# The q, k, v projection joined to layer 0's block, with the attention's first loads beside the value products

## The reference, cut to what matters

```python
xs = layer_norm(ALPHA * xs + g2_s * fs, ln2_g[i], ln2_b[i])        # end of layer 0
hs = xs * (1.0 + sc1_s) + sh1_s                                     # modulation of layer 1
q, k, v = split_heads(h @ w_qkv)                                    # 1024 x 3072, 16 heads of 64
s_loc = einsum('bhrjqd,bhrjkd->bhrjqk', qb, kg) + bias              # window keys, relative position bias, mask
s_ctx = einsum('bhrjqd,bhkd->bhrjqk', qb, k_ctx)                    # 256 cached context keys
p = softmax(concatenate([s_loc, s_ctx]))
o = p[..., :nk] @ vg + p[..., nk:] @ v_ctx
```

## Time and profile before

| what | value |
|---|---|
| median of 3 runs | 3832.96 us (3830.51 to 3836.11) |
| the profiled execution, its own time | 3835.01 us |
| its span | 3833.2 us |
| TensorE matmuls busy | 3599.0 us, 94% of the span |
| mean granted clock of TensorE | 0.974 of full |
| last matmul of layer 0's feed-forward to the first projection matmul | 1943 to 1976.10 us |
| projection | 1976.10 to 2325.7 us |
| last value matmul to the first minimum of the attention | 2325.7 to 2355.61 us |

### The profile page before, as it was taken

The page is one execution under the profiler, slowest core; times in us unless marked ns, Lnnn a source line. Parts: engine busy times, 40 slices in busy tenths (PEclk is TensorE's granted clock), DMA queues, the critical chain, the costliest instruction groups (busy, mean ns, idle before and its releaser), DMA issues. The chain is left out here.

```text
span 3833.2 us, 47327 instructions
## 1 busy us (share of the span) xinstructions
PE 3599.0 (94%) x19244; PEld 3066.8 (80%) x19244; DVE 1515.4 (40%) x2472; ACT 1034.0 (27%) x1552; POOL 1229.6 (32%) x815
## 2 busy tenths in 40 slices
PE   8999998889999999999979996999899999999997
PEld 7788887667788888888858876888778888888886
DVE  2765553454434443344440013777331122211116
ACT  1441211132511111111242213777434111111113
POOL 1531113533522222222351212666253222222223
PEclk9999999899999999999989998999999999999998
DMA  3253324754122222222243436777211111111111
GB/s 117 94 171 111 106 88 159 241 170 149 45 66 67 81 68 72 66 66 66 72 146 134 150 124 177 172 180 178 88 34 33 39 39 39 39 34 39 39 39 61
DMA packets 178567, 369.58 MB, mean 96 GB/s; under 512 B 17048, under 2 KB 102552, under 8 KB 176697
## 3 DMA queue, kind: packets, MB, share of 16 engines
q1 hardware_dynamic: 172920, 356.21, 29.2%
q10 hardware_dynamic: 5440, 10.49, 0.9%
HBM read 286.93 MB, written 79.69 MB: 96 GB/s over the span
## 5 line engine op out<-in xcount | busy, mean ns | idle before, releaser
L147 POOL TENSOR_TENSOR w_lo<-w_raw,w_hi 128x1024 fp32r<-128x1024 f32 x210 | 505.6, 2408 | 1513.7 <-ACT w_hi L141 1513.7
L155 PE MATMUL ps_r<-a_hi,w_hi 128*128 128x512 f32 (+1 forms) x2112 | 539.3, 358 | 13.0 <-POOL a_lo L1440 10.6
L155 PE MATMUL ps_r<-a_hi,w_lo 128*128 128x512 f32 (+1 forms) x2112 | 535.8, 357 | 0.0
L155 PE MATMUL ps_r<-a_lo,w_hi 128*128 128x512 f32 (+1 forms) x2112 | 535.6, 357 | 0.0
L141 ACT ACTIVATE w_hi<-w_raw 128x1024 fp32r<-128x1024 f32 (+1 forms) x217 | 225.2, 1038 | 1024.9 <-PE ps_r L155 442.3
L155 PEld LDWEIGHTS ps_r<-a_hi,w_hi 128*128 128x128 f32 x2112 | 350.9, 188 | 84.0 <-POOL a_lo L1440 18.2
L155 PEld LDWEIGHTS ps_r<-a_hi,w_lo 128*128 128x128 f32 x2112 | 350.8, 188 | 62.5
L155 PEld LDWEIGHTS ps_r<-a_lo,w_hi 128*128 128x128 f32 x2112 | 350.9, 188 | 62.4 <-issue 1.0
L1632 DVE TENSOR_TENSOR hid_l<-hid_l,ps_r 128x1280 f32<-128x1280 f32 x44 | 65.5, 1488 | 843.0 <-PE ps_r L155 843.0
L1652 DVE SCALAR_TENSOR_TENSOR x_t_l<-ps_r,mod,x_t_l 128x1024 f32<-128x1024 f32 (+1 forms) x288 | 241.4, 880 | 266.0 <-PE ps_r L155 266.0
L1480 POOL TENSOR_TENSOR hid_lo_l<-hid_l,hid_hi_l 128x1280 fp32r<-128x1280 f32 x42 | 134.6, 3205 | 490.7 <-ACT hid_hi_l L1382 490.7
(11 more groups left out here) (232 smaller groups left out, 6517.7 us busy)
## 6 DMA issues: line engine op xcount, KB each, us to landing
w_raw<-in_w_all SPq DMA_DIRECT2D x213, 512.0 KB, 3.6
ada_w_l<-in_ada_t SPq DMA_DIRECT2D x59, 512.0 KB, 3.6
q_hl<-q_d SPq DMA_DIRECT2D x64, 320.0 KB, 5.9
v_hl<-v_d SPq DMA_DIRECT2D x128, 128.0 KB, 2.9
t_tail_f<-in_ada_t SPq DMA_DIRECT2D x24, 512.0 KB, 4.1
k_hl<-k_d SPq DMA_DIRECT2D x32, 384.0 KB, 8.8
spec<-gout_f SPq DMA_DIRECT2D x80, 128.0 KB, 2.1
g_spec_c<-spec ACTq DMA_DIRECT2D x20, 512.0 KB, 5.3
```

The source lines that it names most:

```text
L147: pool.tensor_tensor(wl[:, s, 0:width], raw[:, s, 0:width], wh[:, s, 0:width].bitcast(F32), ALU.subtract).then_inc(w_split, 1)
L155: last = pe.matmul(out[:, c0:c1], w[:, c % 2, blk * 128:blk * 128 + 128], x[:, c0:c1], start=start and b == 0 and term == 0, stop=stop and ...
```

## The change

The five engine parts of `stage_qkv` become functions (`qkv_parts`) that run at the end of `stage_rest(0)`'s own block, with tiles laid over those that the LayerNorm no longer needs. So no barrier stands between the two. The first two weights' products are made chunk by chunk: the first two chunks of both, then the third, which waits for `a_lo` k by k. ACT and POOL wait for the stores of x (`y_out`) before they write over `x_t`. The value blocks are taken in the order 8, 9, 0, ..., 7 (`VM`), so that the additional copies to `z_f` fall on the first four halves. After the third value block SP loads q, k and bias of the attention's first head, after the fourth, fifth and sixth a third of the mask each, which ACT converts. The last stores of v are no longer awaited at the end of the block, but by SP in the attention ahead of the loads of v. The attention's first head waits for no load, and its prologue on ACT runs one tiny exponential first. A few small tiles move into the arena, and the first head's q, k, mask and bias tiles are shared by the two stages. What is computed is the same.

```diff
+        def load_qk(sp, q, k, pair, hh, q_done, k_done):
...
+        def qkv_parts(st, e0, place, pg, px, n2, y_out):
+            vwh, vwl = [place(n, 32768 * b, [128, KT, D], F32R) for b, n in enumerate(("vw_hi", "vw_lo"))]
+            zf = place("z_f32", 65536, [128, 2, TOK])
+            zh, zl = [place(n, 75776 + 10240 * b, [128, 2, TOK], F32R) for b, n in enumerate(("z_hi", "z_lo"))]
+            zv = [place(f"z_v{n}", 76288 + 8192 * n, [128, 8, 2, 128], F32R) for n in range(2)]
+            pv = [px[:, 0:512], px[:, 512:1024]]
+            VM = (8, 9, 0, 1, 2, 3, 4, 5, 6, 7)
+            att = first_att(place)
...
+            def qkv_sp(sp):
+                sp.wait_ge(n2.acc, 24)
+                cache_in(0)
+                cache_in(1)
...
+                for n, m in enumerate(VM):
+                    sp.wait_ge(vl_ok, 2 * n + 2)
+                    sp.dma_start(v_d[128 * m:128 * m + 128, :, :, :], zv[n % 2].bitcast(F32)).then_inc(v_out[n % 2], 16)
+                    if n < 2:
+                        sp.wait_ge(vf_ok, 2 * n + 2)
+                        sp.dma_start(t["nv"][128 * m - LS:128 * m - LS + 128, :], zf[:, n, 0:1024]).then_inc(c_out, 16)
+                    if n == 2:
+                        for j in range(2):
+                            sp.wait_ge(z_out[j], 1 + 32 * 4 + 48 * 4)
+                        sp.wait_ge(c_out, 16 * 14)
+                        load_qk(sp, q0, k0, 0, 0, q_e, k_e)
+                        sp.wait_ge(w_split, EV + 10)
+                        load_bias(sp, bias, 0, 0, b_e)
+                    if 3 <= n < 6:
+                        if n > 3:
+                            sp.wait_ge(ms_ok, n - 3)
+                        sp.dma_start(m_raw[:, :], t["mask"].rearrange("p a b -> p (a b)")[:, 768 * (n - 3):768 * (n - 2)]
+                                     ).then_inc(ms_in, 16)
+                sp.wait_ge(q_e, 64)
+                sp.wait_ge(k_e, 32)
+                sp.wait_ge(b_e, 128)
...
+            def qkv_pool(pool):
+                pool.wait_ge(y_out, 16 * 24)
+                pool.wait_ge(n2.bc, 3)
...
+            def qkv_act(act):
+                act.wait_ge(y_out, 16 * 24)
...
+                for n in range(20):
+                    m, h = n // 2, n % 2
+                    if n in (12, 14, 16):
+                        c = n // 2 - 6
+                        act.wait_ge(ms_in, 16 * c + 16)
+                        act.activation(att[2].rearrange("p a b -> p (a b)")[:, 768 * c:768 * c + 768], m_raw[:, :],
+                                       ACT.Copy).then_inc(ms_ok, 1)
...
+                    if m < 2:
+                        act.activation(zf[:, m, 512 * h:512 * h + 512], pv[h][:, :], ACT.Copy).then_inc(vf_ok, 1)
...
+                    if m < 2:
+                        dve.wait_ge(vf_ok, n + 1)
...
+            def qkv_pe(pe):
+                pe.wait_ge(n2.acc, 24)
+                for j in range(2):
+                    pe.wait_ge(w_split, e0 + j + 1)
+                    if j:
+                        pe.wait_ge(n2.s2_ok, 21)
+                    for ci in range(2):
+                        pe.wait_ge(n2.lo, 8 * ci + 8)
+                        products(pe, e0 + j, [(k, a_h[:, k, :], a_l[:, k, :], pg[j]) for k in range(KT)],
+                                 (CHUNKS[ORDER[ci]],))
+                for j in range(2):
+                    for k in range(KT):
+                        pe.wait_ge(n2.lo, 16 + k + 1)
+                        last = products(pe, e0 + j, [(k, a_h[:, k, :], a_l[:, k, :], pg[j])], (CHUNKS[ORDER[2]],),
+                                        k == 0, k == KT - 1)
+                    last.then_inc(w_used, 1)
...
+                        c0 = 128 * VM[m]
+                        xh, xl = a_h[:, k, c0:c0 + 128], a_l[:, k, c0:c0 + 128]
...
@@ stage_rest, at the end of each engine's part
+                    if not last_layer:
+                        qkv_sp(sp)
...
-        def stage_qkv(e0):
...
-        stage_qkv(e0)
@@ the attention's stage
+            q0, k0, mask, bias = shared[0]
+            qq = [q0, place("q_hl1", 76288, [128, 2, TOK], F32R)]
+            kk = [k0, place("k_hl1", 86528, [128, 1536], F32R)]
...
-                load_qk(0, 0)
-                flat = t["mask"].rearrange("p a b -> p (a b)")
-                for n in range(2):
-                    if n:
-                        sp.wait_ge(mk_ok, 1)
-                    sp.dma_start(pb[:, :, :].rearrange("p a b -> p (a b)")[:, 0:1152],
-                                 flat[:, 1152 * n:1152 * n + 1152]).then_inc(m_in, 16)
-                    if n == 0:
-                        load_bias(0, 0)
+                for j in range(2):
+                    sp.wait_ge(v_out[j], 16 * 5)
                 for n in (0, 4, 1, 2, 3, 5):
                     load_v(0, n)
-                load_qk(0, 1)
-                load_bias(0, 1)
+                load_qk(sp, qq[1], kk[1], 0, 1, kq_in[1], kq_in[1])
+                load_bias(sp, bias, 0, 1, b_in[1])
...
+                    first = i * 96 + 96 * (u // U) + 96 * hh
+                    if u % 10 == 0 and first:
+                        pe.wait_ge(kq_in[hh], first)
...
                 def prologue():
-                    for n in range(2):
-                        act.wait_ge(m_in, 16 * n + 16)
-                        act.activation(mask[:, :, :].rearrange("p a b -> p (a b)")[:, 1152 * n:1152 * n + 1152],
-                                       pb[:, :, :].rearrange("p a b -> p (a b)")[:, 0:1152], ACT.Copy).then_inc(mk_ok, 1)
+                    act.activation(stat[:, 0, 3:4], eps[:, :], ACT.Exp)
...
-                    pool.wait_ge(mk_ok, 2)
```

More of the change, by code:

```diff
@@ L996, in hyena_natten_step, with first_att, names_of @@
         ORDER = (2, 0, 1)
+        shared = []
+        def first_att(place):
+            return (place("q_hl0", 92672, [128, 2, TOK], F32R), place("k_hl0", 70144, [128, 1536], F32R),
+                    place("mask", 65536, [128, 6, 384], BF16),
+                    nc.alloc_sbuf_tensor_at(names_of("rpb_t"), [128, 2, 16, RPB_W], F32, offset=base_w).ap())
+        def names_of(name):
+            names[0] += 1
+            return f"{name}_{names[0]}"
+        def load_qk(sp, q, k, pair, hh, q_done, k_done):
+            rows = slice(64 * hh, 64 * hh + 64)
+            for hl in range(2):
+                for half in range(2):
+                    sp.dma_start(q[64 * half:64 * half + 64, hl, :].bitcast(F32), q_d[hl, pair, rows, :]).then_inc(q_done, 16)
+            for hl in range(2):
+                sp.dma_start(k[64 * hl:64 * hl + 64, :].bitcast(F32), k_d[hl, pair, rows, :]).then_inc(k_done, 16)
@@ L1291, in _ @@
                     spread(n2, 2)
+                    if not last_layer:
+                        qkv_pe(pe)
                 @block.scalar
@@ L1895, in hyena_natten_step @@
+                    if not last_layer:
+                        qkv_dve(dve)
         stage_rest(0, e0)
         e0 += E_OUT + E_FFN
-        stage_qkv(e0)
         e0 += E_QKV
@@ L2057, in _ @@
                     load_v(i, 3)
-                    load_bias(i, 1)
+                    load_bias(sp, bias, i, 1, b_in[1])
             @block.tensor
@@ L2078, in scores @@
                         for hl in range(2):
-                            last = pe.matmul(dst, qq[:, hh, hl, c0:c0 + 128], keys, start=hl == 0, stop=hl == 1)
+                            last = pe.matmul(dst, qq[hh][:, hl, c0:c0 + 128], keys, start=hl == 0, stop=hl == 1)
                     last.then_inc(s_mm, 1)
@@ L2203, in bias_mask @@
                         pool.wait_ge(sm_ok, unit_at(i, u - 1))
-                    if u % 10 == 0:
-                        pool.wait_ge(b_in[hh], i * 128 + (128 * (u // U) + 128))
+                    first = i * 128 + 128 * (u // U) + 128 * hh
+                    if u % 10 == 0 and first:
+                        pool.wait_ge(b_in[hh], first)
                     x = BIAS_X[j]
```

431 lines of the change are left out of this document (192 added, 239 removed).

## The result

The changed kernel takes 3808.8 us as the median of five runs (3807.8 to 3812.5). The kernel before took 3836.1 beside it, the median of five (3830.5 to 3843.2). The ratio is 0.9931 [0.9918, 0.9944], so 27 us are gained where 34.45 were forecast, and the median lies 10 us above the forecast of 3798.6, at the very top of the range of 3791 to 3809. Repeated twice beside other kernels, the changed kernel had 3806.2 and 3810.2, the one before 3837.1 and 3837.0.

The account below looks back on a forecast made before the run. TensorE, busy 94% of the span, was taken as the bound, so only its idle time could be won. 12.2 - 0.55 + 25.6 - 2.8 = 34.45 us saved gave a median of 3798.6 us, range 3791 to 3809.

Parts of the forecast that it names:

- the low clock at the third tile: Projection's third tile, after PE's wait for its weight: a low-clock start was taken as 0, with 2.75 us as bound.
- the second head's late loads: Attention's change to the second head: v, q, k and bias queue behind the awaited store, 2.8 us lost, bounds 0 and 7.2.
- the third weight's low part will end at 1994.65: First border: cache chain and third weight's load shift earlier together; third tile starts at 1994.65 instead of 2006.85, 12.2 us saved.
- the wait of 2.55 us: Projection: PE, done with two tiles at 1992.1, waits 2.55 us for the third weight until 1994.65.
- The value products: Value products: an extra copy lengthens the wait ahead of the third half, 0.55 us lost; new loads hide at no cost.
- The second border: Value products to attention: first minimum at about 2330.0 instead of 2355.61, 25.6 us saved, last-copy part included.
- at 231 GB/s that is 22.7 us: Attention start: 5.24 MB from v to the second head's last bias take 22.7 us, so bias comes 23.6 after the first minimum.
- all that it is later is paid: Change to the second head: bias 23.6 us after the first minimum instead of 20.8, the whole 2.8 us lost.
- the first head's half pair starves, or PE falls to the low clock in the 2.55 us wait: Rival: second head's loads 7.2 us late, or low clock at the third tile; 27.3 us saved with both; chance 0.23.
- The faster flow: Rival: loads flow at 333 GB/s and the third weight's chain hides, 39.8 us saved, 3793.2; chance 0.12.
- the single border: Rival: attention finds its first k or bias missing, so only the first border is won, 3821.3; chance 0.07.
- The held stores of v: Rival: SP's mask-copy waits hold back value-block stores beyond 11.7 us of slack; 16 us slower, 3849.1; chance 0.04.

Follow-up runs that it names:

- merge: Only the first border changed against the kernel before; attention loads and the wait for the stores of v left as before: 3824.8 us, ratio 0.9968.
- again: The changed kernel run once more, with no edit: 3806.2 us, ratio 0.9921 to the kernel before.
- bias: Against the changed kernel, the second head's bias is loaded among the value products, behind the mask: 3806.2 us, ratio 0.9924 to the kernel before.
- thirdbias: Against the changed kernel, third projection weight's load and splits moved earlier and second head's bias loaded among the value products: 3800.9 us, ratio 0.9911 to the kernel before.
- qkbias: Against the changed kernel, second head's bias loaded among the value products, its q and k ahead of v: 3811.4 us, ratio 0.9934 to the kernel before.
- third: Against the changed kernel, third projection weight loaded ahead of the cache loads, its splits ahead of the last cache splits: 3800.7 us, ratio 0.9905 to the kernel before.
- vmiddle2: Second run: against the changed kernel, third weight first, second head's bias early, its q and k amid v's loads: 3795.7 us, ratio 0.9897 to the kernel before.

## Where the forecast held, and which steps failed

**In short.** The direction and the mechanism of both borders held. Two terms of the sum failed: the low clock at the third tile, put at 0, cost 1.3 to 1.5 us, and the second head's late loads, put at 2.8 us, cost 6.3 to 7.4. The start of the attention took 0.85 us more than summed.

**The borders.** The first: "the third weight's low part will end at 1994.65" is 35.35 us after the mark; it ended 35.06 after it. The third tile started 12.35 us earlier than the row that the forecast took for its start, forecast 12.2. Merge shows the border alone, 11.9 against 11.65 to 12.2. The reading that this chain shifts as a whole with the cache loads, and that it is the next bound, held.

**The clock at the third tile was the first miss.** The step that failed is the wait of 2.55 us, and with it "I take 0, since 2.55 is nearest to the 2.52 of the row". The wait was 3.3, 4.1 and 3.9 us in the three executions: PE was ready 31.9, 31.0 and 30.9 us after the mark, forecast 32.8 (1992.1). The first product runs 1.08 us behind the spread's start (1962.87 less 1961.79 in again), where the forecast had it wait for the spread's end at 2.08, and the two tiles took 30.8 us from there in the first execution and 29.9 in again, for the forecast's 30.75. Behind each of these waits the clock fell, which cost 1.3 to 1.5 us (16.75, 16.60 and 16.71 from the tile's start to its copy, for the 15.26 of bias), within the bound of 2.75. In bias the same wait was 2.92 us, and the clock stayed at 1.00. So here the two rows that the forecast went by fit, and the length of the wait put in was what failed; with the tiles' start and duration open by 2 us, that step should have had a range and not one value.

**The value products** held. The third half waited 4.8, 4.1 and 4.1 us, forecast 4.1; from the fifth on the halves are 5.44 us apart, no store of v held anything, and the last value split is 12.4 us earlier after the mark (355.22 against 367.60), forecast 12.2. So what the clock had cost was made up on the way: a projection tile took 13.92 us in this execution and 14.00 in the kernel before, and behind the third half's wait 9 matmuls ran at the low clock, where it was 13 before. In again (14.00 us a tile, 12 such matmuls) the split was 11.7 earlier. That the first execution met the forecast here is luck in part.

**The second border** came at 359.72 after the mark, forecast 359.06 (396.31 less 12.2, plus 0.55, less 25.6). From the last split of the value products to the first minimum it took 4.5 us, not the 3.65 of the sum: 0.85 us. Of it 0.4 lie between the end of the split (2320.03) and POOL's first work of the attention (2321.92), which the sum had at 1.5 us, and the rest from there to the minimum; why was not tried.

**The second head was the large miss.** The term of 2.8 us measured 6.3, 6.9 and 7.4. The first step that failed is "at 231 GB/s that is 22.7 us". The rate was right: the 25.17 us from the first load of v to the second head's bias ran at 232 GB/s. But a rate times the bytes of the wanted tiles is not the time until the last of them can be used. The trace of before held the same row of loads, from its first issue at 2349.33 to the bias at 2376.40: 27.07 us, with the second half of the mask (0.6 MB, issued at 2348.94) still on its way at its start. At that stretch's 238 GB/s the mask is 2.5 us, which leaves 24.6. In the changed kernel the row took 25.2, 25.4 and 26.0. At 232 GB/s 25.2 us are 5.8 MB, 0.6 more than the wanted 5.24; the two loads of the next pair's v, 0.5 MB, are issued at 2340.96 while the bias is still on its way, and the third head's q and k (2.1 MB) from 2341.91 on. How much of the 2.5 us is that of these loads and how much the last load's own latency was not separated. The second step that failed is "all that it is later is paid": it was too little. The bias came 25.3 us after the first minimum, forecast 23.6, before 20.8. So it was 4.5 later than before, and F to H grew by 6.3 (6.9 and 7.4 in the others). The sum had no term for k, which by the run bias is some 2 us of it, and none for the low clock behind the waits, which the last fence of the second border shows; what that clock alone costs there was not separated from the bias. The forecast's upper bound of 7.2 was near, but was argued from another mechanism, the whole shift of the queue passed on.

The rule of the Trainium skill that the forecast set beside this (DMA: Bandwidth & Descriptors, Specifications, some 358 GB/s for one core) does not describe this stretch: 232 GB/s at a DMA share of 0.98. Nor is it a bound elsewhere in this trace: 410 GB/s in the window from 2000 to 2003. It was right not to use it.

**The sum, for the first profiled execution.** From the mark to the end 30.9 us are saved (1873.9 to 1843.0), forecast 34.45. The differences by step are +0.2 up to the last value split, -0.85 to the first minimum, -3.5 to the third head, +0.6 in all that follows. The other 6.8 us of the 10.4 between 3798.6 and this execution's own 3808.96 are in no step of the sum: 4.8 are the later mark, and 2.0 the step from a profiled execution to the median. The median of three runs that the forecast ended on was 3833.0; with more runs it is 3836 to 3837.

**The rivals.** What happened is the first one, "the first head's half pair starves, or PE falls to the low clock in the 2.55 us wait", with both of its parts: 27.3 saved was its number; 27.3, 30.9 and 26.8 were measured by the medians of three sets, and 30.3, 29.3 and 29.0 from the mark to H. It had a chance of 0.23 and should have had more than the forecast: one of its parts lay 1 us of wait away, and for the other the trace of before held a row of loads 2 us longer than the 22.7. The faster flow fell with the 232 GB/s, the single border with merge. The held stores of v did not show in any profile.

Left open: the order of the value blocks was not tried alone, since the mask and k are loaded over the tile that the copies of the new tokens use.

## What to carry to other kernels

When a row of loads is moved, take its duration from the trace of the same row of loads, first issue to first use, less what else was on its way there, and not from a rate (24.6 us for the 25.2 to 26.0 measured; the rate gave 22.7); and put the price of a low clock on every new wait of 2 us or more, as a range, since here such waits went either way. A fused border has a next bound in each queue that it joins: here moving a load to the front helped only when the splits behind it moved too, and loads that compete for a full queue should stand in the order in which they are needed. Compare executions from the last row that the change leaves alone; here its place alone differed by up to 6 us between executions.

## What the runs showed of the hardware

- A wait of TensorE of 2 to 3 us can go either way. At the third tile the granted clock fell behind waits of 3.30, 3.32, 3.83, 3.85, 4.03, 4.04 and 4.10 us and stayed at 1.00 (the high level, 2.4 GHz) behind 2.92. Among the short units of the attention it fell to 0.50 (the low one, 1.2 GHz) behind single waits of 1.98 (thirdbias) and 2.36 us (qkbias) and behind two waits close together, 1.55 and 2.23 (the changed kernel) and 2.01 and 2.03 (third), and stayed behind 2.16 (vmiddle2) and 2.34 (bias). In some executions the first three matmuls after the wait were still quick (three in 0.84 us in the changed kernel, where again has 1.43 for three at the low level) and the fall came behind them. The Trainium skill (TensorE: Matmul & The Clock Gate, What's actually happening) says that the slow clock is the resting state and activity lifts it; the traces agree with that (before the change the projection starts at 0.50 behind its wait of 14.7 us and is at 1.00 from 1982 to 1985), and show that the length of the last wait alone does not tell which level follows where the engine was only partly busy ahead of it.
- Loads of v, q, k and bias kept the DMA engines at a share of 0.98 to 0.99 with 228 to 232 GB/s over 25 us, while cache and weight traffic reached 346 to 410 GB/s at a share of 1.09 to 1.15. What makes the difference was not tried.
- One execution of thirdbias took 3785.0 us, its others 3800 to 3804. In its profile the whole difference lies behind H (1416.8 us against 1431 to 1437), in the feed-forward, where 110 us hold 578 matmuls instead of 568, at a granted clock of 1.00 in both:

```profile
2916.42:3026.42 110.00, 110.00 (x578) 94.26 (x577) 17.88 (x19) 15.34 (x14) 27.98 (x11) 1.00 0.12 39
```
```profile
2923.92:3033.92 110.00, 110.00 (x568) 93.28 (x567) 17.88 (x19) 15.34 (x14) 27.93 (x11) 1.00 0.12 36
```

The first line is thirdbias, the second the changed kernel. TensorE was 1.8% quicker there with nothing in the rows that says why; its cause stays open.
